# Weighted sum of expert rows with the diagonal stationary, coefficients two rows behind their dot product, and two adaLN tiles earlier in the load queue

## The reference, cut to what matters

```
mod  = silu(c) @ w_ada + b_ada                # adaLN: sh1, sc1, g1, sh2, sc2, g2, 1024 numbers each
x    = x + g1 * token_mixer(modulate(x, sh1, sc1))
h    = modulate(x, sh2, sc2)                  # rmsnorm(x) * (1 + sc2) + sh2
q    = h @ w_q                                # 8 heads; keys give 2 x 128 scores, top 16 of the sums
for token, head:                              # 16 experts e with gates p (softmax of their scores)
    y += p[e] * gelu(h . u[e]) * v[e]         # u[e], v[e]: rows of 1024 numbers
out  = x + g2 * y
```

## Time and profile before

| | |
|---|---|
| median of 3 runs | 2688.87 us (2685.58 to 2690.92) |
| profiled execution, its own time | 2693.61 us |
| its span, first to last instruction | 2691.3 us |
| mean granted TensorE clock | 0.975 |
| TensorE busy | 2496.1 us (93%) |
| VectorE busy | 2076.1 us (77%) |
| ScalarE busy | 1255.4 us (47%) |
| GpSimd busy | 266.2 us (10%) |
| the gathers' queue (q0) | 268.45 MB, 24.3% of 16 DMA engines |

### The profile page before, as it was taken

One profiled execution on the slowest core, in us unless ns is written; L12 is line 12 of the kernel. 1 busy time (PEld: TensorE's weight loads), 2 busy tenths in 40 slices (PEclk: granted clock), 3 DMA queues, 4 the chain that ended last, 5 costly groups with the idle time before them and its releaser, 6 DMA issues.

```text
span 2691.3 us, 38029 instructions
## 1 busy us (share of the span) xinstructions
PE 2496.1 (93%) x14586; PEld 2159.8 (80%) x14586; DVE 2076.1 (77%) x3119; ACT 1255.4 (47%) x1542; POOL 266.2 (10%) x286
## 2 busy tenths in 40 slices
PE   5999999999999999999999998998998999887787
PEld 4789997787888888888888887757788898877676
DVE  6768984856898989898998983636758887887875
ACT  3234443236777777767777763102333333332322
POOL 0000001000000000000000000000002344333331
PEclk9989999989999999999999998999988999999999
DMA  8647775556999999999999966214548999999997
GB/s 348 249 174 279 275 291 205 195 220 257 356 356 354 354 356 356 339 350 357 351 357 354 354 242 234 102 42 193 228 164 312 411 420 420 420 420 420 420 420 307
DMA packets 109562, 824.92 MB, mean 307 GB/s; under 512 B 11896, under 2 KB 15224, under 8 KB 16128
## 3 DMA queue, kind: packets, MB, share of 16 engines
q1 hardware_dynamic: 71792, 551.75, 53.9%
q0 software_dynamic: 36864, 268.45, 24.3%
q10 hardware_dynamic: 720, 2.24, 0.2%
HBM read 821.34 MB, written 1.05 MB: 306 GB/s over the span
## 4 chain that ended last, share of the span: by engine, by line
PE 73%; DMA 13%; DVE 7%; issue 4%; ACT 1%; POOL 0%; SPq 0%; DVEq 0%; ACTq 0%; another core or an unknown queue 0%; POOLq 0%
PE ps L700 14%; PE ps L702 14%; PE ps L701 14%; DMA ring<-in_uv,arena 10%; PE ps L686 7%; PE ps L764 5%; PE ps L1489 4%; PE ps L719 4%; DMA arena<-in_uv,arena 3%; PE ps L694 2%; PE ps L1353 1%; PE ps L924 1%; PE ps L936 1%; PE ps L1400 1%; PE ps L1081 1%
## 5 line engine op out<-in xcount | busy, mean ns | idle before, releaser
L1827 DVE TENSOR_TENSOR ring_r<-ring,arena_r 128x2048 fp32r<-128x2048 f32 x336 | 770.2, 2292 | 11.4
L2254 ACT ACTIVATE arena_r<-ring 128x2048 fp32r<-128x2048 f32 x378 | 725.8, 1920 | 29.6 <-DMA ring<-in_ffn_w_down 13.1
L700 PE MATMUL ps<-arena_r 128*128 128x512 f32 (+1 forms) x1120 | 417.2, 373 | 1.5 <-DVE arena_r L1863 1.5
L702 PE MATMUL ps<-arena_r 128*128 128x512 f32 x896 | 349.3, 390 | 0.0
L701 PE MATMUL ps<-ring_r,arena_r 128*128 128x512 f32 x896 | 348.6, 389 | 0.0
L1489 PE MATMUL ps<-sel,ring 128*128 128x128 f32 x2272 | 280.6, 280 | 61.2 <-ACT sel L2254 59.2
L1489 PEld LDWEIGHTS ps<-sel,ring 128*128 128x128 f32 x2272 | 265.1, 193 | 74.0 <-ACT sel L2254 70.6
L2254 ACT ACTIVATE sel<-cs,arena 128x128 f32<-128x128 f32 x256 | 102.9, 402 | 414.5 <-DVE arena L2206 383.8
L1489 PE MATMUL ps<-sel,arena 128*128 128x128 f32 x1824 | 230.0, 282 | 44.4 <-ACT sel L2254 43.4
L1489 PEld LDWEIGHTS ps<-sel,arena 128*128 128x128 f32 x1824 | 215.8, 195 | 55.6 <-ACT sel L2254 55.2
L2254 ACT ACTIVATE arena<-ps 128x512 f32<-128x512 f32 (+2 forms) x208 | 103.4, 497 | 295.6 <-PE ps L686 93.2
(11 more groups left out here) (285 smaller groups left out, 3881.8 us busy)
## 6 DMA issues: line engine op xcount, KB each, us to landing
ring<-in_moe_w_gate SPq DMA_DIRECT2D x112, 1024.0 KB, 5.0
ring<-in_moe_w_up SPq DMA_DIRECT2D x112, 1024.0 KB, 5.0
ring<-in_moe_w_down SPq DMA_DIRECT2D x112, 1024.0 KB, 5.0
ring<-in_ada_w SPq DMA_DIRECT2D x24, 1024.0 KB, 9.8
ring<-in_ada_w SPq DMA_DIRECT2D x12, 2048.0 KB, 8.0
ring<-in_w_in SPq DMA_DIRECT2D x10, 2048.0 KB, 12.5
ring<-in_w_ada SPq DMA_DIRECT2D x8, 2048.0 KB, 8.0
ring<-in_ffn_w_gate SPq DMA_DIRECT2D x14, 1024.0 KB, 5.1
```

What stands on the lines that cost most here:

```text
L700: e.matmul(out, xs[0], ws[0], start=start, stop=False, skip_group_check=True)
L702: return e.matmul(out, xs[1], ws[0], start=False, stop=stop, skip_group_check=True)
L1827: v(e.tensor_tensor(ring_low[ring.half[unit]], ring.buf[unit], mo.high[unit_at[unit] % NHIGH].bitcast(F32), ALU.subtract), ("low", unit))
L2254: A.mark(e.activation(out, src, func, **kw), name)
```

## The change

Six things are done, all visible in the diff:

- `pe`: a row is two matmuls (`c` in 0, 1) with the diagonal stationary and 512 columns of v moving, so that the sum builds up as tokens by channels.
- `act` and `pe` get new work at rows 33 to 43: `x_tokens(t)` turns xT to tokens by channels (8 transposes and 2 copies of 128x512 for each half, written over xT), and `gate_tokens` spreads g2 over the partitions (8 matmuls of 128x128 and 2 copies of 128x512, into `m.scr[:, 0:1024]`).
- `dve`: `sums(t)` is four operations of 128x512 (two multiplications, two additions) in place of eight of 128x128; `sp` and the host read the output as tokens by channels, for half 1 from `m.scr`.
- `dve` does coefficient(i - 2) after dots(i), and `act` does diagonal(i - 1) after gelu(i). So row i reaches TensorE once the dot product of row i + 2 is done.
- `added(1, n)` moves from rows 0, 1 to rows 1, 2; `normed(1, ...)` from 10, 11 to 13, 14, and ScalarE's `peer_shift(1, ...)` from 12, 13 to 14, 15.
- `sp` loads adaLN tiles 2 and 3 ahead of `w_in2` 4096.

```diff
--- before.py
+++ after.py
@@ -633,11 +633,11 @@
             slot(s[2])
             for n in range(2):
                 load_half(("w_hy", n), T["w_hy"][n])
-            slot(s[3])
-            load(("w_in2", 4096), T["w_in2"][8])
             for at, t in ((s[0], ada[2]), (s[1], ada[3])):
                 slot(at)
                 load_ada(t)
+            slot(s[3])
+            load(("w_in2", 4096), T["w_in2"][8])
             e.wait_ge(*P["hyena done"])
             e.wait_ge(*V["hyena done"])
             e.dma_start(na_tile(0), T["w_na"][0]).then_inc(in_na[0], 16)
@@ -665,10 +665,14 @@
             e.wait_ge(*P["w_na", 1, 0])
             e.dma_start(pq_tile(3)[:, 2048:4096], T["w_pq"][3][:, 2048:4096]).then_inc(in_pq3[0], 16)
 
-            for t, k in ((0, 0), (0, 4), (1, 0), (1, 4)):
-                e.wait_ge(*V["out", t, k])
-                e.dma_start(T["out"][t].rearrange("p (k j) -> p k j", k=8)[:, k:k + 4, :],
-                            xT[:, k:k + 4, 128 * t:128 * t + 128]).then_inc(out_stored[0], 16)
+            for k in (0, 4):
+                e.wait_ge(*V["out", 0, k])
+                e.dma_start(T["out"][0].rearrange("p (k j) -> p k j", k=8)[:, k:k + 4, :],
+                            xT[:, k:k + 4, 0:128]).then_inc(out_stored[0], 16)
+            for k in (0, 4):
+                e.wait_ge(*V["out", 1, k])
+                e.dma_start(T["out"][1][:, 128 * k:128 * k + 512],
+                            pr.scr[:, 1024 + 128 * k:1536 + 128 * k]).then_inc(out_stored[0], 16)
             e.wait_ge(*out_stored)
 
 
@@ -1459,6 +1463,21 @@
                     b = bank(("tokens", t, q), (4 + 2 * t + q,))
                     P.mark(turned(b, [hT[:, 4 * q + k, 128 * t:128 * t + 128] for k in range(4)]), ("tokens", t, q))
 
+            def x_tokens(t):
+                for q in range(2):
+                    e.wait_ge(*V["x", "second", t, q])
+                    b = bank(("x tokens", t, q), ASIDE[2:])
+                    P.mark(turned(b, [xT[:, 4 * q + k, 128 * t:128 * t + 128] for k in range(4)]), ("x tokens", t, q))
+
+            def gate_tokens():
+                for q in range(2):
+                    b = bank(("gate tokens", q), ASIDE[2:])
+                    for k in range(4):
+                        last = e.matmul(b[:, 128 * k:128 * k + 128],
+                                        mod[2][:, 40 + 4 * q + k:41 + 4 * q + k].to_broadcast([128, 128]), ident,
+                                        start=True, stop=True)
+                    P.mark(last, ("gate tokens", q))
+
             keys = ring.buf["keys"]
             some(na1, 1)
             key_scores(0)
@@ -1481,15 +1500,18 @@
                     query(*ASKED[i])
                 if i in SCORED:
                     key_scores(SCORED[i])
+                if i in (33, 37):
+                    x_tokens((i - 33) // 4)
+                if i == 41:
+                    gate_tokens()
                 if i == 123:
                     tokens(1)
                 e.wait_ge(*A["diag", i])
                 rows = row_buffer(i)[0]
-                for c in range(8):
-                    last = e.matmul(ps.banks[2 * t + c // 4][:, 128 * (c % 4):128 * (c % 4) + 128],
-                                    rows[:, 1024 + 128 * c:1152 + 128 * c], m.diag[:, i % NDIAG, :],
-                                    start=(i % 128 == 0 and c % 4 == 0), stop=(i % 128 == 127), skip_group_check=True)
-                    if i % 128 == 127 and c == 3:
+                for c in range(2):
+                    last = e.matmul(ps.banks[2 * t + c], m.diag[:, i % NDIAG, :],
+                                    rows[:, 1024 + 512 * c:1536 + 512 * c], start=(i % 128 == 0), stop=(i % 128 == 127))
+                    if i % 128 == 127 and c == 0:
                         P.mark(last, ("first half", t))
                 P.mark(last, ("rows", i))
 
@@ -2208,12 +2230,13 @@
 
             def sums(t):
 
-                c = slice(128 * t, 128 * t + 128)
-                for k in range(8):
-                    e.wait_ge(*(P["first half", t] if k < 4 else P["rows", 128 * t + 127]))
-                    b = ps.banks[2 * t + k // 4][:, 128 * (k % 4):128 * (k % 4) + 128]
-                    v(e.scalar_tensor_tensor(xT[:, k, c], b, mod[2][:, 40 + k:41 + k], xT[:, k, c], ALU.mult, ALU.add),
-                      ("out", t, 4 * (k // 4)))
+                e.wait_ge(*A["x tokens", t])
+                e.wait_ge(*A["gate tokens"])
+                for q in range(2):
+                    e.wait_ge(*(P["rows", 128 * t + 127] if q else P["first half", t]))
+                    x, y = xT[:, 4 * q:4 * q + 4, 128 * t:128 * t + 128], m.scr[:, 1024 + 512 * q:1536 + 512 * q]
+                    v(e.tensor_tensor(y, ps.banks[2 * t + q], m.scr[:, 512 * q:512 * q + 512], ALU.mult))
+                    v(e.tensor_tensor(v4(y, 4) if t else x, x, v4(y, 4), ALU.add), ("out", t, 4 * q))
 
             for _ in choices(0, 0):
                 pass
@@ -2228,14 +2251,14 @@
                                          m.dots[:, i:i + 1]), ("dots", i))
                 if i % 16 == 0:
                     gates(*HEADS[j])
-                if i:
-                    coefficient(i - 1)
-                if i in (0, 1):
-                    added(1, i)
+                if i > 1:
+                    coefficient(i - 2)
+                if i in (1, 2):
+                    added(1, i - 1)
                 if i == 8:
                     rstd(("norm_peer", 1), m.scr[:, 2049:2050])
-                if i in (10, 11):
-                    normed(1, range(4 * i - 40, 4 * i - 36))
+                if i in (13, 14):
+                    normed(1, range(4 * i - 52, 4 * i - 48))
                 if i % 16 == (4 if j else 9):
                     for _ in later:
                         pass
@@ -2244,7 +2267,8 @@
                     next(later, None)
                 if i == 140:
                     sums(0)
-            coefficient(255)
+            for i in range(254, 256):
+                coefficient(i)
             sums(1)
 
 
@@ -2653,6 +2677,17 @@
                     a(m.sbufs[t][h], v4(b[:, 256 * n:256 * n + 256], 2), ACT.Copy, ("pscore", t, h))
                 emptied(("pscore", j))
 
+            def x_tokens(t):
+                for q in range(2):
+                    a(xT[:, 4 * q:4 * q + 4, 128 * t:128 * t + 128], v4(taken(("x tokens", t, q)), 4), ACT.Copy,
+                      ("x tokens", t))
+                    emptied(("x tokens", t, q))
+
+            def gate_tokens():
+                for q in range(2):
+                    a(m.scr[:, 512 * q:512 * q + 512], taken(("gate tokens", q)), ACT.Copy, "gate tokens")
+                    emptied(("gate tokens", q))
+
             def exp_gates(t, h):
                 gate = m.gate[t][:, 16 * h:16 * h + 16]
                 e.wait_ge(*V["margins", t, h])
@@ -2680,8 +2715,12 @@
                 if i == 8:
                     exp_gates(*HEADS[1])
                     root(("norm_peer", 1), ps.bank["norm_peer", 1][:, 0:1], D, pr.scr[:, 2049:2050])
-                if i in (12, 13):
-                    peer_shift(1, range(4 * i - 48, 4 * i - 44))
+                if i in (14, 15):
+                    peer_shift(1, range(4 * i - 56, 4 * i - 52))
+                if i in (35, 39):
+                    x_tokens((i - 35) // 4)
+                if i == 43:
+                    gate_tokens()
                 if i in QUERIED:
                     query(QUERIED[i])
                 if i - 2 in SCORED:
@@ -2689,7 +2728,9 @@
                 if i % 16 == 8 and 8 < i < 240:
                     exp_gates(*HEADS[i // 16 + 1])
                 gelu(i)
-                diagonal(i)
+                if i:
+                    diagonal(i - 1)
+            diagonal(255)
 
 
 
@@ -2900,4 +2941,4 @@
     program(nc, T)
     res = run_bass_kernel_spmd(nc, [ins], core_ids=[0])
     return np.ascontiguousarray(
-        res.results[0]["out_x"].reshape(2, 128, 8, 128).transpose(0, 3, 2, 1).reshape(1, 256, 1024))
+        res.results[0]["out_x"].reshape(1, 256, 1024))
```

## The result

| | runs | median, us | ratio to before, 95% interval |
|---|---|---|---|
| before | 17 | 2689.98 | |
| changed kernel | 17 | 2694.10 (2692.09 to 2696.31) | 1.0016 [1.0009, 1.0023] |

The difference is +4.1 us, by the interval +2.4 to +6.2. The median lies 1.1 us above the range of the prediction (2682 to 2693), and the kernel is slower where it was forecast to be a little faster. By the prediction's own line for "slower", 5.4 us, the +4.1 still counts as "same", which it gave 0.74; but the interval leaves out zero.

The account below looks back on a forecast made before the run. From 2100 to 2665 us the full DMA engines bound the row stage. The terms -0.6 - 0.7 - 1.2 + 1.6 = -0.9 us took the profiled 2693.61 to 2692.7 us, the median 2688.87 to 2688.0; range 2682 to 2693.

Parts of the forecast that it names:

- adaLN tiles: Attention, ahead of the row stage: loading tile 2 before `w_in2` removes VectorE's 0.64 us wait, gain 0.6 us (0 to 0.64).
- the onset: First rows, up to gather 21: row 13 starts on TensorE 0.7 us sooner, gain 0.7 us (ends -5.8 and +4.0).
- full stretch: Rows from 2100 to 2665 us, DMA engines full: gathers issued one row later still land in time, cost 0.
- instruction packets: TensorE's instruction loads on the DMA engines: 70% of packets go, 1.2 us less to carry (ends 0 and 1.9).
- the end: Behind the last dot product: three rows wait instead of two, sums slightly shorter, +1.6 us (ends 1.2 and 2.0).
- Three stalls should go: VectorE in the first rows: waits of 1.49 (`added`), 1.51 and 1.00 us (coefficient) vanish, together 4.0 us; 3.70 stay.
- over rows 0 to 15 I take 3.3: First rows: the lag brings row i to TensorE one dot product later, priced at 3.3 us for a VectorE row.
- The slack of 7.5 us: Full stretch: gather 33 had 10.5 us and would need 3.0 alone, so the lag's 2.5 to 3.97 us fits.
- Rival 1: End of transfer: TensorE's packets all lie on the engine ending last, so 8 us are gained, 2680.6; chance 0.08.
- Rival 2: Rows 24 to 53: buffers starve, onset 2.5 us later, two bursts at 1.5; +5.3, 2694.2; chance 0.15.
- Rival 3: Onset: the whole gain of 5.8 us, with TensorE's full clock and a free lag; -6.0, 2682.9; chance 0.10.
- Rival 4: TensorE rows cheaper by the skill's ratio: end -1.5 in place of +1.8, shorter row 13; 2683; chance 0.05.

## Why the prediction was wrong

| step | forecast, us | what the runs showed |
|---|---|---|
| adaLN tiles | -0.6 | the wait of 0.64 is gone; not seen in a median |
| the onset | -0.7 | +1.1 to +1.8 at the last dot product |
| full stretch | 0 | about +0.5 |
| instruction packets | -1.2 | a quarter of the packets; no gain in time seen |
| the end | +1.6 | +1.2: the lag +1.7 to +1.85, the form -0.4 |
| sum | -0.9 | +4.1 (+2.4 to +6.2) |

**The step that failed is "The onset".** It had the sign wrong: 0.7 us sooner was forecast, and gather 21 goes out 1.3 to 3.2 us later than in the usual profiles of the old order. Three of its terms were wrong.

First, the gain: "Three stalls should go ... together 4.0 us". The 1.49 us went. The 1.00 us could not go, since it is the wait of a selection and not of a coefficient, which I misread. The 1.51 us hang on ScalarE, which was itself waiting for a projection on TensorE, 3.35 us in before and 5.49 in after. In three of the five profiles with the lag in the first rows, those with row 1 at 1.2 GHz, 1.95 to 1.98 us of stall stand there, and in the other two 0.39 and 0.45. So the stalls that went were worth 1.0 to 2.6 us and not 4.0.

Second, the price of the lag: "over rows 0 to 15 I take 3.3" us for a row. This is the term that fails in all five profiles. The mean is of no use here: row 13 hangs on one dot product, number 15, and the intervals ahead of it are the heaviest, 4.78 and 5.05 us, since the change itself put `normed` there. Behind the first gather VectorE reached dot product 14 at 62.7, where it was 65.6 in the kernel without a lag, but dot product 15 only at 67.4. Row 13 waited for the first of these dates and now for the second: 1.9 us later. It started at 69.4 us in after, and at 67.3 to 67.7 in all seven profiles with the old order in the first rows. In the two profiles in which the coefficient's stall nearly went, dot product 14 is reached at 61.1 and 61.3 and dot product 15 at 65.9 and 66.1, and row 13 starts at 67.9 and 68.0: the price of 4.8 us takes up the whole gain there, where 0.7 us were to be left. The forecast called `normed` free because its operations stay the same; it was put in the interval on which the lag made TensorE depend.

Third, the row's length. I took row 13 at 3.78 us as a property of the kernel. Of those seven profiles, it runs at 2.4 GHz in five (1.98 to 2.05 us) and at 1.2 GHz in two (3.78), one of them the profile before. In all five with the lag there it stands behind 2.7 to 2.8 us of idle time and takes 3.0 to 3.3 us, at a mean granted clock of 0.57 to 0.64. With the usual row in place of the one I saw, gather 21 goes from 69.8 or 70.0 to 73.0 in three profiles, and to 71.3 and 71.4 in the two with the small stall.

These dates do not pass to the end one for one, which was the premise of the step ("what gather 21 gains the end gains"). The three that are 3.0 to 3.2 us late there are 1.8 to 2.3 us late at the last dot product, and the two that are 1.3 and 1.6 us late are 2.2 and 1.6. The share from 40 to 85 us and gathers 15 and 32 are worse in all five; which of the late gathers costs how much is open, and so is the part of the moved operations. In the full stretch the forecast had the cost at 0, where about 0.5 us was measured; that belongs to the same lag.

**What was right.** The bound and the rule that came from it: the full stretch is a transfer, and neither TensorE's shorter loads nor the added transposes moved it (the form alone has its last dot product at 673.3); nearly all that was lost or gained lies at the onset and the end. The slack of 7.5 us covered the lag but for the half microsecond: dot product 64 to 255 takes 485.8 and 485.4 us in the two profiles of after, 485.3 and 486.0 in those of before. The end was nearly right, +1.2 to +1.3 for +1.6. The 1.79 us for a row more are confirmed (1.7 and 1.85); what I took too low was what the form gives back, 0.4 instead of 0.15.

**Instruction packets.** The size of the traffic was right: 16 packets to 4 in 320 us, 117 to 93 in the program. The time is not shown. From dot product 64 to 255 the forecast would be 1.0 us less (1.2 x 485 / 590). The four profiles of the old form have 485.3 to 486.4 us, the ten of the new form 484.5 to 486.4: the gain is smaller than that spread, or none. The end of the transfer suggests why. These are the 5 us from 10 to 5 us ahead of the last dot product, in the second profile of before and in after:

```profile
2667.92:2672.92 5.00, 4.17 (x35) 3.79 (x34) 2.78 (x6) 1.21 (x4) 0.00 (x0) 1.00 0.36 152
```

```profile
2669.75:2674.75 5.00, 4.06 (x9) 1.35 (x8) 2.77 (x6) 1.21 (x4) 0.00 (x0) 1.00 0.11 48
```

The share is 0.31 to 0.42 in all four profiles of the old form and 0.08 to 0.11 in all ten of the new one. Over the last 15 us it is 0.39 to 0.43 against 0.28 to 0.33, about 0.1 of 15 us, or 1.5 us of all the engines' time: the work that was to be saved is of that size. But in the last 5 us the share is 0.07 and 0.05, about what one engine of 16 is (0.06), and the rows land at 2.46 us from each other in both forms. My 1.2 us took the mean over 16 engines, while the last landing, as these shares have it, goes by the last of them. That it is the packets, and not something else of the new form, which frees the others is not shown. The rule of the Trainium skill (Runtime: NRT & Kernel Launch, Instruction fetch mechanics), that the cost is mostly hidden, fits at least as well as my 1.2 us.

**The rivals.** Rival 1 (the last engine, -8): excluded; the form alone leaves a quarter of the packets, and its last dot product is at 673.3 where the second profile of before has 673.2. What ends sooner are the other engines. Rival 2 named 2694.2, close to the result, but for another reason: of its two bursts at 1.5 us each only some 0.5 us is there, while its later onset does exist, at 1.1 to 1.8 us for 2.5. A number that fits does not confirm a mechanism. Rival 3 needed a lag that costs nothing, and failed as said there, since each coefficient waits for a further dot product. Rival 4, the cheaper rows: a row alone takes 1.98 us as 4 instructions of 512 columns and 2.05 as 16 of 128, and two rows in one go 3.60 (after) and 3.74 (the lag alone, in the old form). By the ratio of the Trainium skill (TensorE: Matmul & The Clock Gate, Back-to-back issue gap), 131 ns against 4 times 81, the first would be 0.4 of the second. It is 0.96. For these f32 products the trace decides: columns cost, not instructions.

**The range** missed by 1.1 us. The ends that the step itself had worked out (-5.8 to +4.0 for the onset) held the result; the range gave the upper end only half of rival 2. With +2 for the onset and the rest of the forecast the sum would have been +1.8, inside the range.

The sum of the parts by the marks, 3.0 to 3.6 us against the second profile of before, lies 0.5 to 1.1 under the medians' 4.1, within their interval. What is made ahead of the first gather can't be told: its date differs by 1.8 us between the two profiles of the unchanged kernel (2006.51 and 2004.71), and lies anywhere from 2001.2 to 2006.5 in the 14 profiles.

## What to carry to other kernels

A stage that a transfer bounds is gained and lost mostly at its two edges, and a software pipeline with one row more of distance pays at both: at the end, one row's time behind the last landing; at the start, for each item the interval on which its buffer hangs, so look up those intervals (here 4.78 us for row 13) and not the mean (3.3), and what the change itself moved into them. Before a stall is counted as gained, look at what its releaser was waiting for: here the stall went or stayed with TensorE's clock in one row. Moving the work that stands in the way gained 2.6 us at the onset, and a shorter distance in the last rows 1.4. Compare profiles from a mark at the start of the stage, with a second profile of the unchanged kernel beside them, before anything is read from a single row's duration.

## What was not expected of the hardware

- The same instructions in the same order ran row 13 at either clock level: 3.78 us in one profile of before, 2.05 in the other, and gather 21 went out 1.7 us apart for it, while by the last dot product 0.9 us of that were left.
- Row 1 did the same in the kernels with the lag: 3.78 us at a granted clock of 0.50 in three profiles, 1.98 and 2.05 us at 1.00 in two. That moved gather 21 by 1.6 us, and the last dot product by nothing that can be seen (675.0 to 675.5 in the three, 674.8 and 675.4 in the two).
- The DMA engines finish far from together. In the last 5 us ahead of the last dot product they carry a share of 0.05 to 0.07, about one engine of 16, and still the last dot products follow each other at 2.46 us, nearly the distance of the full stretch. The mean share over a fixed window says little here: from 2665 to 2680 it is 0.47 and 0.27 in the two profiles of before, but 0.43 and 0.40 in the 15 us ahead of the last dot product, since their first gathers are 1.8 us apart. If the last rows wait for one engine, that would be the next thing to gain; it was not tried.
